# A two-layer sequence model on one core: the key-value boundary in two blocks of time steps, value tiles first

## The reference, cut to what matters

```python
x = x + short_conv_mixer(rmsnorm(x, mix_norm[0]), ...)      # stage "a"
x = x + conv_ffn(rmsnorm(x, ffn_norm[0]), ...)              # stage "f0"
kv = nsa_shared_kv(rmsnorm(x, kv_norm), ...)                # stage "b": keys, values, compression
x = x + nsa_mixer(rmsnorm(x, mix_norm[1]), w_qg, w_o, kv, rel_bias)   # stage "b": queries, attention, output
x = x + conv_ffn(rmsnorm(x, ffn_norm[1]), ...)              # stage "f1"
out = rmsnorm(x, final_norm)                                # "end"
```

## Time and profile before

| | |
|---|---|
| median of 3 runs | 619.44 us (619.2 to 619.78) |
| the profiled execution | 619.53 us, span 617.8 us, mean granted TensorE clock 0.997 |
| TensorE matmuls | 604.2 us busy, 98% of the span |
| TensorE weight loads | 530.5 us, 86% |
| VectorE | 482.2 us, 78% |
| ScalarE | 390.6 us, 63% |
| GpSimd | 57.5 us, 9% |

### The profile page before, as it was taken

The page is one execution under the profiler, slowest core; times in us unless marked ns, Lnnn a source line. Parts: engine busy times, 40 slices in busy tenths (PEclk is TensorE's granted clock), DMA queues, the critical chain, the costliest instruction groups (busy, mean ns, idle before and its releaser), DMA issues.

```text
span 617.8 us, 11378 instructions
## 1 busy us (share of the span) xinstructions
PE 604.2 (98%) x3764; PEld 530.5 (86%) x3764; DVE 482.2 (78%) x955; ACT 390.6 (63%) x727; POOL 57.5 (9%) x81
## 2 busy tenths in 40 slices
PE   9999999999999999999999999999999999999995
PEld 8999997988888888887989877778988888888884
DVE  4888656788888887886877899938788888888765
ACT  7546336766666666667657598737766666666644
POOL 0100011000000000003110156600100000000010
PEclk9999999999999999999999999999999999999998
DMA  8797432355555655781467401023465655555521
GB/s 331 297 342 245 172 136 102 127 214 203 198 198 203 199 199 199 264 288 58 134 205 238 154 2 36 15 94 133 134 213 206 200 194 204 201 191 202 196 102 68
DMA packets 30352, 109.55 MB, mean 177 GB/s; under 512 B 3387, under 2 KB 3659, under 8 KB 30188
## 3 DMA queue, kind: packets, MB, share of 16 engines
q1 hardware_dynamic: 29756, 106.97, 49.4%
q0 software_dynamic: 560, 2.12, 1.0%
HBM read 108.01 MB, written 1.07 MB: 177 GB/s over the span
## 4 chain that ended last, share of the span: by engine, by line
PE 90%; DVE 4%; ACT 2%; issue 1%; DMA 1%; POOL 0%; SPq 0%; DVEq 0%; ACTq 0%
PE bank L1260 24%; PE bank L1264 12%; PE bank L1209 10%; PE bank L1210 10%; PE bank L1211 10%; PE bank L1228 10%; PE bank L1233 5%; PE bank L1305 2%; PE bank L1318 1%; PE bank L1598 1%; DMA bias<-in_xT 1%; DVE work L1132 1%; ACT work L559 1%; PE bank L1555 1%; PE bank L1623 1%
## 5 line engine op out<-in xcount | busy, mean ns | idle before, releaser
L819 DVE TENSOR_TENSOR w<-staged,w 128x1024 fp32r<-128x1024 f32 x188 | 229.2, 1228 | 45.0 <-ACT w L555 44.8
L555 ACT ACTIVATE w<-staged 128x1024 fp32r<-128x1024 f32 x196 | 198.9, 1047 | 21.2 <-PE bank L1211 7.1
L1260 PE MATMUL bank<-gx,w 128*128 128x512 f32 x640 | 159.4, 391 | 0.0
L1260 PEld LDWEIGHTS bank<-gx,w 128*128 128x128 f32 x640 | 117.5, 188 | 23.0 <-DVE work L955 0.2
L1264 PEld LDWEIGHTS bank<-gx,w 128*128 128x128 f32 x640 | 87.3, 190 | 6.2
L1264 PE MATMUL bank<-gx,w 128*128 128x256 f32 x640 | 89.2, 282 | 0.0
L1209 PE MATMUL bank<-w,y 128*128 128x512 f32 x208 | 81.5, 392 | 0.0
L1210 PE MATMUL bank<-w,y 128*128 128x512 f32 x208 | 81.5, 392 | 0.0
L1211 PE MATMUL bank<-w,y 128*128 128x512 f32 x208 | 80.9, 389 | 0.0
L685 ACT ACTIVATE work<-work,params 128x256 f32<-128x256 f32 x96 | 44.2, 504 | 54.0 <-DVE work L955 39.2
L699 ACT ACTIVATE y<-work 128x256 fp32r<-128x256 f32 x52 | 21.7, 418 | 77.8 <-DVE work L976 59.7
(11 more groups left out here) (182 smaller groups left out, 795.8 us busy)
## 6 DMA issues: line engine op xcount, KB each, us to landing
staged<-in_f_up SPq DMA_DIRECT2D x88, 512.0 KB, 5.2
staged<-in_f_down SPq DMA_DIRECT2D x44, 512.0 KB, 3.6
staged<-in_a_up SPq DMA_DIRECT2D x24, 512.0 KB, 7.1
staged<-in_b_up SPq DMA_DIRECT2D x24, 512.0 KB, 4.3
staged<-in_a_down SPq DMA_DIRECT2D x8, 512.0 KB, 3.5
staged<-in_b_down SPq DMA_DIRECT2D x8, 512.0 KB, 4.3
bias<-bias_rows POOLq DMA_DIRECT2D x1, 2048.0 KB, 12.6
x<-in_xt SPq DMA_DIRECT2D x1, 1024.0 KB, 10.0
```

The costliest lines, as they stand in the source:

```text
L555: nc.scalar.activation(w_hi[:, q["slot"], 0:n], staged[:, s, 0:n], ACT.Copy).then_inc(hi, 1)
L819: nc.vector.tensor_tensor(w_lo[:, q["slot"], 0:n], staged[:, s, 0:n], w_hi[:, q["slot"], 0:n].bitcast(F32), ALU.subtract).then_inc(lo, 1)
L1260: nc.tensor.matmul(dst, w_hi[:, s, kt * P:kt * P + P], gx[:, kt, :], start=kt == 0, stop=False, skip_group_check=True)
```

## The change

- `B_ORDER` puts the four `val` pieces first, then `cmp`, then `key`; `w1` follows directly on the last `key`.
- The boundary from f0 to b uses `norm_halves`, and `turn_half` in place of `turn_x`, with no `KEEP_WARM` matmuls. TensorE turns block 0, runs all value matmuls of block 0 (`values(0)`, with the transposes of block 1 ahead of its last quarter), and then `values(1)`. `cmp_pair` goes; `cmp` pieces go through `product`.
- The last two down products of f0 go through `last_downs`, in the order: unit 20 on three banks, then unit 21 on the first two and the third bank, then both on the fourth.
- The last step of f0 is `last_step`: the two channels one after the other in operations of 256 columns in place of one of 512 for both.
- The low part of the last down piece is made by VectorE in the middle of step 20; its leading part moves to there too. The leading parts of b's pieces 2 and 3 move behind `last_step`, and so does the low part of piece 2.
- In b, the low part of the first token block moves from entry 7 to entry 11 of VectorE's loop, its leading part from entry 6 to entry 10 of ScalarE's. Banks of the pairs, the values and the queries change with it.

```diff
-B_ORDER = ([("cmp", t) for t in range(4)] + [("key", t) for t in range(4)] + [("val", t) for t in range(4)]
+B_ORDER = ([("val", t) for t in range(4)] + [("cmp", t) for t in range(4)] + [("key", t) for t in range(4)]
...
-            rest("f0", "down", FU - 1, 0)
...
+            def last_step(st):
+
+                k = FU - 1
+                r, at = k % 3, UP[st] + 2 * (k % 2)
...
+                from_bank(0)
+                tapped_2(0)
+                from_bank(1)
+                act.wait_ge(convolved[st], 4 * k + 2)
+                nc.scalar.activation(conv[:, r, 0, :], conv[:, r, 0, :], ACT.Silu).then_inc(silued[st], 1)
+                tapped_2(1)
+                act.wait_ge(y_done[st], k + 1)
...
+                    if st == "f0":
+                        step(st, FU - 2, (nxt[1:2], [(st, "down", FU - 1, 0)], []))
+                        last_step(st)
+                        for q in nxt[2:]:
+                            lead(*q)
+                        return
...
-            norm("b", meanwhile=B_PIECES(4, 6))
+            norm_halves("b", meanwhile=B_PIECES(4, 6))
...
-                if b in (6, 12):
-                    j = 0 if b == 6 else 1
+                if b in (10, 12):
+                    j = 0 if b == 10 else 1
...
-                if b in (7, 12):
-
-                    j = 0 if b == 7 else 1
+                if b in (11, 12):
+
+                    j = 0 if b == 11 else 1
...
+            def values(tt):
+
+                for t in range(4):
+                    q = piece_of("b", "up", B_ORDER.index(("val", t)), 0)
                     pe.wait_ge(lo_up, q["n"] + 1)
...
+                    if tt == 0 and t == 3:
+                        turn_half("b", 1)
+                    for kk in range(2):
+                        kt = 2 * t + kk
+                        pe.wait_ge(gx_lo_done, split_of("b", tt, kt))
...
-            turn_x("b")
-            cmp_pair(0)
-            cmp_pair(1)
+            turn_half("b", 0)
+            values(0)
+            values(1)
```

More of the change, by code:

```diff
@@ L664, in norm_halves @@
                     lead(*WHILE_O[-1])
-                preload(ACT.Silu)
-                for q in meanwhile:
+                    preload(ACT.Silu)
+                for n, q in enumerate(meanwhile):
                     lead(*q)
+                    if st == "b" and n == 0:
+                        act.wait_ge(gx_lo_done, split_of(st, 1, KT - 1))
+                        for kt in range(KT):
+                            nc.scalar.activation(gq_hi[:, kt, :], turned_x(st, kt), ACT.Copy, scale=gain("mix1", kt)).then_inc(gq_hi_done, 1)
             def step(st, k, ahead, i=0):
@@ L895, in norm @@
                 for kt in range(KT):
[L896 removed]
+                    dve.wait_ge(gx_hi_done, 8 * k + kt + 1)
                     nc.vector.scalar_tensor_tensor(gx_lo[:, kt, :], turned_x(st, kt), gain(GAIN_OF[st], kt),
                                                    gx_hi[:, kt, :].bitcast(F32), ALU.mult, ALU.subtract).then_inc(gx_lo_done, 1)
[L899 removed]
+                for q in meanwhile:
                     rest(*q)
[L901 to L905, removed]
             def norm_halves(st, meanwhile):
@@ L934, in norm_halves @@
                 rests(1)
-                for q in meanwhile:
+                for n, q in enumerate(meanwhile):
                     rest(*q)
+                    if st == "b" and n == 0:
+                        dve.wait_ge(gq_hi_done, 8)
+                        for kt in range(KT):
+                            nc.vector.scalar_tensor_tensor(gq_lo[:, kt, :], turned_x(st, kt), gain("mix1", kt), gq_hi[:, kt, :].bitcast(F32),
+                                                           ALU.mult, ALU.subtract).then_inc(gq_lo_done, 1)
             def step(st, k, ahead, i=0):
@@ L1000, in stage @@
                     step(st, FU - 3, (early, middle, late + nxt[0:1]))
-                    step(st, FU - 2, (nxt[1:2], nxt[2:3], []))
-                    step(st, FU - 1, NOTHING)
+                    if st == "f0":
+                        step(st, FU - 2, (nxt[1:2], [(st, "down", FU - 1, 0)], []))
+                        last_step(st)
+                        rest(*nxt[2])
+                    else:
+                        step(st, FU - 2, (nxt[1:2], nxt[2:3], []))
+                        step(st, FU - 1, NOTHING)
             nc.vector.memset(table_sb[BUCKETS:BUCKETS + 1, :], NEG).then_inc(table_done, 1)
@@ L1449, in stage @@
                     up_f(st, FU - 1)
-                    for k in range(FU - 3, FU):
-                        down(st, k)
+                    down(st, FU - 3)
+                    if st == "f0":
+                        last_downs(st)
+                    else:
+                        down(st, FU - 2)
+                        down(st, FU - 1)
             pe.wait_ge(consts_done, 1)
@@ L1513, in _ @@
                 s = q["slot"]
-                if what == "key":
-                    if b == 6:
-                        pe.wait_ge(b_evacuated, 2)
+                if what in ("cmp", "key"):
+                    if (what, t) == ("key", 0):
+                        pe.wait_ge(vals_done, 2)
                     product(q, pair_bank(b), gx_hi, gx_lo, b % 2 == 0)
@@ L1536, in _ @@
                 pe.wait_ge(lo_up, q["n"] + 1)
-                if what == "val":
+                if what == "w1":
+                    j = t // 2
                     if t == 0:
                         pe.wait_ge(gq_lo_done, 8)
[L1542 to L1549, removed]
                     if t % 2 == 0:
```

88 lines of the change are left out of this document (52 added, 36 removed).

## The result

| | before | after |
|---|---|---|
| median | 619.38 us (6 runs, 618.92 to 619.99) | 623.43 us (6 runs, 621.94 to 625.8) |
| ratio to before | | 1.0073, 95% interval 1.006 to 1.0087 |
| profiled execution, its span | 619.53, 617.8 us | 623.34, 621.5 us |
| mean granted TensorE clock | 0.997 | 0.994 |

The kernel is slower by 4.05 us between the medians (623.43 over 619.38 is 1.0065; the ratio in the table, with its interval, is not that of the medians). The sign is as forecast and the time is inside the stated range; the likeliest case said 2.9 us, and 623.43 lies above the 620.9 to 622.9 that this case spanned alone. The six executions after are spread over 3.9 us, those before over 1.1 us: 621.94, then three from 623.34 to 623.48, then 625.28 and 625.8. The one at 621.94 has the mean clock that the kernel before has (0.997).

What follows compares the result with a forecast made beforehand. The prediction took TensorE's own pace plus its gaps to bound the kernel. Boundary -0.3 and new wait +3.2 gave +2.9 us on the profiled 619.53, 622.4, taken as 622.3 us for the median; range 620.2 to 624.6.

Steps and rivals of the forecast that it cites:

- the likeliest case: Whole kernel: boundary gain and new wait at w1 make it 2.9 us slower, 620.9 to 622.9; chance 0.69.
- the rival with the clock: At w1: TensorE's clock falls in the wait, up to 2.9 us more, 624 to 625 us; chance 0.10.
- The wait at w1: Behind the last key piece: TensorE stands about 3.2 us for VectorE's low part of token block 0.
- The boundary: From f0 to b: two blocks with block 1's transposes give a net gain of about 0.3 us, bounds 0 and 1.4.
- y(21) just arrives: End of f0: y(21) whole at about 283.5, TensorE wants it at 283.6; nothing booked, 0.3 us as bound.
- a clock below 1 behind the wait: Behind the wait at w1: listed among the profile signs that would show the prediction wrong.
- Its price for slow matmuls: Warm-up records at 0.228 us each taken as 1.2 GHz; up to 5.9 us at half rate loses up to 2.9.
- Given back: In the attention: its waits on GpSimd, 2.6 us, shrink, giving 622.3 - 1.7 = 620.6 us; chance 0.10.
- No wait at w1: At w1: block's low part made before the last key piece ends; 619.1 or 618.0 us; chance 0.09.
- GpSimd excludes VectorE: At b's boundary: first residual sums wait for GpSimd's piece 3, first square at 288.1, 624 us; chance 0.02.
- The low part on VectorE: Last down piece, end of f0: its low part had cost GpSimd nothing anyone waited for; on VectorE it is inside the chain.

Runs made afterwards that it cites:

- e1: Changed kernel with the low part of token block 0 moved ahead of VectorE's wait for the last key pair: 618.62 us against 619.37.
- e3: Changed kernel with the low part of piece 17 put ahead of the block's low part in VectorE's list: 624.76 us against 619.37.
- e7: e5 with the square root's table loaded by ScalarE inside the last step of f0: 618.05 us against 619.57.
- e9: e5 with an added GpSimd operation of the low part's size, result unused, near 275 us: 621.96 us against 619.33.
- e2: Changed kernel with twelve matmuls on ones in TensorE's wait ahead of the first w1 piece: 623.46 us against 619.37.
- e5: e1 with five matmuls on ones ahead of block 0's transposes at the boundary from f0 to b: 618.75 us against 619.57.
- e6: e2 with five matmuls on ones at the boundary from f0 to b too: 622.12 us against 619.57.
- e8: e5 with the last down tile's low part made by GpSimd again: 619.77 us against 619.57.
- e4: e1 with the boundary from f0 to b in one block as before, values behind it: 619.79 us against 619.37.

## Why the prediction was right, and where its sizes were off

- **The sign and the cause** were right. That 623.43 lies inside the range is owed to the rival with the clock, whose far side widened the range to 624.6; the likeliest case's own bounds ended at 622.9.
- **The wait at w1** was right in place, cause and size: 3.2 us foretold, 3.30 measured between the matmuls, 2.95 us of VectorE's four operations foretold, 2.96 in the trace. e1 took it away by moving that one instruction, e3 made it longer by 1.14 us.
- **The boundary** was right: net gain 0.3 us foretold, 1.34 - 0.88 = 0.46 in the profile. ScalarE's queue was the limit, as worked out: the wait for the down piece, two leads, the table. The first square came 0.49 us ahead of the last down matmul's start (285.79, 286.28); the prediction had 0.46 (286.35, 286.81). e7 shows the limit by lifting it.
- **y(21) just arrives**: nothing booked, 0.3 us as the bound; the gap ahead of unit 21's matmuls was 0.08 us, and the last three down products took 0.19 us more from first to last start than before (8.17 and 7.98).
- **The clock** was a rival with a chance of 0.10 and belonged into the likeliest case; a clock below 1 behind the wait even stood among the signs of being wrong, and it came. This is the term that was mis-sized: it was booked at nothing, and in the profiled execution it cost 1.58 us at w1. The step behind it set the 3.5 us that passed at the kernel's end before the clock fell beside the 3.1 us of the coming stand, as if a shorter stand kept the clock; but it fell behind the stand of 3.1 us, and in e9 behind one of 2.35. The prediction also priced the removed warm-up matmuls at nothing: e2's profile shows the clock falling at the boundary without them, and with them (e5, e6) none of 16 executions has a mean clock below 0.996. Its price for slow matmuls rested on the pace of the first ones of the kernel, 0.228 us each; the profile gives 1.00 as the granted clock there, so only the pace spoke for 1.2 GHz. Without any fall the changed kernel stands near 622 us: 621.76 for the profiled execution less the 1.58, 622.12 with both gaps filled, against 622.3 foretold. The execution at 621.94, mean clock 0.997, is likely such a one, but the mean does not prove it: one of e2 with the same mean took 623.29.
- **Given back**: 0.21 us behind w1, of the up to 1.7 that the second rival allowed; the attention's waits stayed at 2.6 us. **No wait at w1** and **GpSimd excludes VectorE** at the residual sums did not happen: the first two took 1.28 us together beside GpSimd's low part at 284.81.
- **The low part on VectorE**: the prediction said that on GpSimd it had cost nothing that anyone waited for, and that holds for the kernel before, where it ran from 278.10. But its leading part moved to 275 us, and at that place GpSimd's low part costs about 1.0 us (e8), so the move to VectorE is needed and not merely free. The prediction did not see this, without effect on its total. It told the rule of the Trainium skill, "SBUF — State Buffer", section "Who interferes with whom", more coarsely than the section does, and weighed it by residual sums that read a bank, to which the rule in full does not apply; its sentence that by that rule they would wait is a misreading. The trace of before had operations of the other kind, with both inputs in SBUF, under GpSimd's additions, and they took about twice the 1.2 us of the earlier trace rows. GpSimd's timeline and VectorE's:

```profile
305.53 2.34 POOL L481 TENSOR_TENSOR work<-work,params 128x960 f32<-128x960 f32 x1 [18.45 <-ACT work L737]
```

```profile
306.57 2.38 DVE L819 TENSOR_TENSOR w<-staged,w 128x1024 fp32r<-128x1024 f32 x1 [0.19 <-ACT w L555]
```

Left open: why the clock falls in some executions and not in others, the 0.6 us between the medians of e4 and e1 that their profiles do not show, and about 0.4 of the 1.0 us between e8 and e5 (their profiles differ by 0.56 us at the last matmul).

## What to carry to other kernels

When pieces change their order, follow each engine's list past the move and ask what now stands directly ahead of the bound engine's next need: an instruction that was covered by the moved work may sit behind a wait on that very work. A gap in a dense TensorE stream costs its length and, in some executions, slow matmuls behind it, so a new gap of the size seen here (2.35 and 3.1 us) is booked with the clock, and matmuls on ones are left in until their removal has been timed. Before work moves between GpSimd and VectorE, look at which VectorE operations with both inputs in SBUF it will lie over.

## What the runs showed of the hardware

- TensorE's granted clock fell to 0.50 (1.2 GHz) inside four of the profiled kernels, each time after matmuls had started again: 0.1 us into w1 behind a stand of 3.1 us (changed kernel, for 3.4 us); 0.3 us into w1 behind a stand of 4.3 us (e3); 0.5 us into the values behind a stand of 1.4 us, eight transposes and 0.3 us (e2, from about 290.5 to 293.9); and 0.9 us into unit 21's matmuls behind a stand of 2.35 us (e9). The stretch of e2 passed at 1.00 in three other profiles. For e9, the first matmul behind the stand, and the windows (TensorE busy, granted clock, DMA share, GB/s):

```profile
285.95 0.50 PE L1268 MATMUL bank<-w,y 128*128 128x512 f32 x1 [2.35 <-DVE y L1033]
```

```profile
283.00:286.00 3.00, 0.65 (x4) 1.00 0.00 0
286.00:288.00 2.00, 2.00 (x7) 0.71 0.00 0
288.00:290.00 2.00, 2.00 (x6) 0.50 0.66 211
```

- VectorE, with both inputs in SBUF, and GpSimd hold each other up: 0.42 us became 2.35 and 2.63 us for VectorE, 2.4 became 3.44 us for GpSimd when VectorE was first by 0.05 us.
